# First eight projection tiles on tokens without their norm factor; smaller bias and sum matmuls, in a decoder block on one core

## The chip, the cores and the metric

One Trainium2 chip, one core. The metric is the device time of one execution of the whole program, in microseconds (us). Five engines run their own instruction lists and meet only through semaphores: PE (TensorE, matrix products), DVE (VectorE), ACT (ScalarE), POOL (GpSimd) and SP (SyncE, which here only issues DMAs).

## The reference

A decoder block on 256 tokens of width 1024, in float32:

```
xn = rmsnorm(x) * g1
proj = xn @ w_in                      # 5376 columns: GLU 1024, q, k, v 768 each, gates 2048
conv = layernorm(depthwise_conv31(a * sigmoid(gate))) -> silu -> @ w_proj
attn = dilated attention, 12 heads in 3 groups, scores + rel_bias[bucket(distance)]
h = x + (sigmoid(g_conv) * conv + sigmoid(g_attn) * attn @ w_attn) @ w_out
y = h + PEER(rmsnorm(h) * g2)         # product keys, top 16 of 128x128 experts for 8 heads
```

rmsnorm(x) is x * 1/sqrt(mean(x*x) + 1e-6), with one factor for each token.

## The kernel before

Tokens lie along the free axis: `resid` is [128, 8, 256], 8 blocks of 128 channels by 256 tokens. All weights stream through a ring of four slots of 128x1024 float32 (`raw`). Each weight tile and each right-hand side is cut into a rounded high part and a low remainder, both in the format fp32r, and a product is three matmuls: high by high, high by low, low by high. So a tile costs 24 matmuls of 128x256 (8 blocks by 3).

For a tile, SP issues its DMA when the slot is free (`load`), ACT writes the high part (`split_hi`, L312), then POOL, or DVE for every fourth tile, writes the low part (`split_lo`, L327), and PE multiplies (`product`, L1092). The order on each engine is the order of the code, and nothing overtakes. ACT splits tile n+3 in turn n of the loop over the 42 tiles of `w_in`, ahead of `evac_front(n)`, which reads result n out of PSUM. Tiles 0 to 7 give the GLU (job "glu", gate and value blocks by turns), 8 to 19 give q and k (job "qk"), then v and the gates. PSUM has eight banks; `BANK_OF` gives banks 0 to 5 to the jobs by turns, `start(job)` makes PE wait until the bank's last reader is done (`freed`), and banks 6 and 7 hold the sums of the depthwise convolution, which DVE adds tap by tap from turn 8 (`conv_tap`, L717).

The first norm stands ahead of everything: ACT squares `resid`, DVE adds pairs of blocks, PE sums over channels with a matrix of ones (job "ssq1", L1112), ACT takes the root, DVE the reciprocal. `normalise` then makes xn block by block on DVE (L671), ACT rounds it (`split_norm`, L426) and DVE takes the remainder (L666). PE starts tiles 0 and 1 side by side as the blocks come.

The bias table: 12 matmuls with 33 rows (`bias_row`, L1102) choose each head's bias row and repeat it on all 128 partitions; ACT copies each to `prob`; DMAs write it to DRAM (`toeplitz`) and read it back skewed into `bias`. The layer norm and the second RMS norm sum over channels in the same way, with 4, 4 and 8 matmuls of ones (jobs "lnsum", "lnvar", "ssq2").

After the front come 128 tiles of expert keys and 128 of expert values, with top-16 search on DVE. The change leaves their code alone.

Of the kernel before, what the change touches and what calls it, by code (L numbers as in the profile page):

```python
# [50 lines left out]
WARM_UP = 12  # L51
# [7 lines left out]
BIAS_AT = {1: (7, 8, 9), 2: (10, 11)}  # L59
# [4 lines left out]

TAPS_AT = {}
# [4 lines left out]
def jobs_in_order():  # L70

    order = [(("ssq1",), None)] + [(("bias", h), None) for h in range(7)]
    for n in range(T_CONV):
        if n < T_QK:
            order.append((("glu", n), n))
        elif n < T_V:
# [49 lines left out]
BY_DVE = ("kb", "score", "lnsum", "o", "conv", "attn", "mix")  # L126


def freed_by_dve(job):
    return job[0] in BY_DVE or (job[0] in ("glu", "pT") and job[1] % 2 == 1)  # L130

# [20 lines left out]
def hybrid_block(nc, x_t, front, cols, rel_bias, onehot, sub_keys, u_tiles, v_tiles, out):  # L152
    toeplitz = nc.dram_tensor("toeplitz", (HEADS, P * BW), F32, kind="Internal").ap()
    with ExitStack() as ctx:
# [25 lines left out]
        relb = tmp("relb", [BUCKETS + 1, HEADS, P])  # L180
# [10 lines left out]
        cu_hi = tmp("cu_hi", [P, CB, T], F32R)  # L191
        cu_lo = tmp("cu_lo", [P, CB, T], F32R)
# [6 lines left out]
        o_hi = tmp("o_hi", [P, AB, T], F32R)  # L199
        o_lo = tmp("o_lo", [P, AB, T], F32R)  # L200
# [22 lines left out]
        def part(t0, n):  # L223
# [23 lines left out]
        prm_in, rel_in, bias_out, bias_in, sk_in, y_out = [sem(s) for s in (  # L247
            "prm_in", "rel_in", "bias_out", "bias_in", "sk_in", "y_out")]
# [9 lines left out]
        relb_ready = sem("relb_ready")  # L258
# [64 lines left out]
        def split_lo(eng, base, it, j):  # L323
# [4 lines left out]
               .then_inc(lo_ready[s], 1)  # L328

# [92 lines left out]
        def _(a):  # L422
            def split_norm(k, round_):

                a.wait_ge(normed, KB * round_ + k + 1)
                a.copy(nrm_hi[:, k, :], sq[:, k, :]).then_inc(nhi, 1)  # L426

            def bias_rows(h):
                job_done(a, ("bias", h))
                a.copy(p3[:, h, :], bank[BANK_OF[("bias", h)]][:, 0:BW]).then_inc(act_evac, 1)  # L430
# [10 lines left out]
            split_hi(a, 1, 0, 0)  # L441
            for h in range(3):
                bias_rows(h)
            for k in range(KB):
                split_norm(k, 0)
                if k < 4:
                    bias_rows(3 + k)
            split_hi(a, 2, 0, 0)
# [51 lines left out]
            for n in range(T_CONV):  # L500
                split_hi(a, n + LEAD, 0, 0)
# [147 lines left out]
        def _(dve):  # L649
# [12 lines left out]
            def normalise(gain, round_):  # L662

                def lower(k):
                    dve.wait_ge(nhi, KB * round_ + k + 1)
                    dve.tensor_tensor(nrm_lo[:, k, :], sq[:, k, :], nrm_hi[:, k, :].bitcast(F32), ALU.subtract)\  # L666
                       .then_inc(nlo, 1)

                link(dve.reciprocal(rs[:, 0, 0:T], rs[:, 0, 0:T]))
                for k in range(KB):  # L670
                    dve.scalar_tensor_tensor(out=sq[:, k, :], in0=resid[:, k, :], scalar=prm[:, gain + k:gain + k + 1],  # L671
                                             in1=rs[:, 0, 0:T], op0=ALU.mult, op1=ALU.mult).then_inc(normed, 1)
                    if k:
# [4 lines left out]
            for r in range(2):
                dve.wait_ge(squared, r + 1)
                dve.tensor_tensor(sq[:, 4 * r:4 * r + 2, :], sq[:, 4 * r:4 * r + 2, :], sq[:, 4 * r + 2:4 * r + 4, :],  # L680
                                  ALU.add).then_inc(pair_sums, 1)
                if r == 0:
                    dve.wait_ge(rel_in, 32)
                    dve.wait_ge(const, 1)
                    dve.tensor_copy(relb[:, :, :], relx[:, :].unsqueeze(2).broadcast_to([BUCKETS + 1, HEADS, P]))\
                       .then_inc(relb_ready, 1)
            dve.wait_ge(prm_in, 16)
            dve.tensor_tensor(gains[:, :], prm[:, C_QG:C_QG + 1], prm[:, C_KG:C_KG + 1], ALU.mult).then_inc(gains_ready, 1)
            freed(dve, ("ssq1",))
            normalise(C_N1, 0)  # L690
            for g in range(LEAD):
                lo_of(g)

            def glu(b):

                job_done(dve, ("glu", 2 * b + 1))
                freed(dve, ("glu", 2 * b))
                dve.scalar_tensor_tensor(out=u_pad[:, b, TAPS - 1:], in0=bank[BANK_OF[("glu", 2 * b + 1)]][:, 0:T],
                                         scalar=prm[:, C_GLU + b:C_GLU + b + 1], in1=sig[:, b, :],
                                         op0=ALU.add, op1=ALU.mult).then_inc(dve_evac, 1)  # L700

            def conv_tap(w):

                for b in range(CB):
# [73 lines left out]
            for n in range(T_CONV):  # L778
                lo_of(n + LEAD)
                if n < T_QK and n % 2:  # L780
                    glu(n // 2)
# [21 lines left out]
                if n == WEIGHTS_AT + 1:  # L803
                    group_weights()
                if n == LNSUM_AT + 1:

                    job_done(dve, ("lnsum",))
                    dve.wait_ge(tap, CB * TAPS)
# [5 lines left out]
                    group_factors()  # L814
                if n > LNSUM_AT + 1:
# [45 lines left out]
            for b in range(KB):  # L861
# [3 lines left out]
                   .then_inc(dve_evac, 1)  # L865
            freed(dve, ("ssq2",))
# [611 lines left out]
```

## Time and profile before

| what | value |
|---|---|
| median of 3 runs | 1055.03 us (1053.35 to 1056.5) |
| profiled execution, its own time | 1056.55 us |
| its span (first to last instruction) | 1054.6 us |
| mean granted TensorE clock | 0.993 of 2.4 GHz |
| PE, weight load, DVE, ACT, POOL busy | 98%, 87%, 72%, 50%, 52% |

Busy shares are averages over stages with different limits. The clock of TensorE has two levels, 2.4 and 1.2 GHz, shown as 1.00 and 0.50. Matmuls are pipelined, so a PE that is busy is not always at its full rate.

### The profile page before, as it was taken

The numbers are of one execution on the slowest core, as the hardware profiler recorded it, in microseconds if no ns is written. First come the engines' busy times: TensorE is split into PE (matmuls) and PEld (weight loads), VectorE is DVE, ScalarE is ACT, GpSimd is POOL, SyncE is SP. The second block draws the span as 40 slices with busy tenths as digits, with TensorE's granted clock in tenths as the row PEclk, the third lists the DMA queues.
The fourth block names the chain that finished last, engine by engine and source line by source line (L and its number), as shares of the span: only waits on it lengthen the run. The fifth ranks groups of instructions, "written<-read, shape, count | busy, mean of one in ns | idle before, by whom it ended". The sixth has DMA issues, their size and how long they took to land.

```text
span 1054.6 us, 21139 instructions
## 1 busy us (share of the span) xinstructions
PE 1037.7 (98%) x7338; PEld 921.4 (87%) x7338; DVE 761.0 (72%) x1280; ACT 528.0 (50%) x862; POOL 551.6 (52%) x232
## 2 busy tenths in 40 slices
PE   8999998999999999999999999999999999999998
PEld 6998998999999999999888888877777778888886
DVE  5376887743299999027666666799999997777774
ACT  5454667445454444454555555544444444454453
POOL 3555562655678999984343343443443343444442
PEclk8999999999999999999999999999999999999999
DMA  5864351654545454654544554555455545556552
GB/s 192 263 224 159 108 174 62 221 179 140 180 136 179 155 188 142 216 180 160 176 164 170 173 174 161 179 178 176 162 170 174 174 161 195 188 192 199 195 188 95
DMA packets 52258, 181.91 MB, mean 172 GB/s; under 512 B 5851, under 2 KB 9051, under 8 KB 52092
## 3 DMA queue, kind: packets, MB, share of 16 engines
q1 hardware_dynamic: 52220, 181.41, 52.0%
q8 instruction: 24, 0.39, 0.2%
q14 instruction: 14, 0.11, 0.0%
HBM read 177.97 MB, written 3.41 MB: 172 GB/s over the span
## 4 chain that ended last, share of the span: by engine, by line
PE 87%; DVE 4%; issue 4%; POOL 3%; ACT 1%; DMA 1%; SPq 0%; POOLq 0%; ACTq 0%; DVEq 0%
PE bank L1385 33%; PE bank L1092 29%; PE bank L1327 11%; PE bank L1329 6%; PE bank L1341 3%; POOL lo L327 3%; PE bank L1174 2%; PE bank L1102 1%; PE bank L1303 1%; DVE nrm L1016 1%; DVE gsig L856 1%; PE bank L1251 1%; DMA relx<-rel_bias 1%; PE bank L1190 0%; PE bank L1237 0%
## 5 line engine op out<-in xcount | busy, mean ns | idle before, releaser
L327 POOL TENSOR_TENSOR lo<-raw,hi 128x1024 fp32r<-128x1024 f32 x218 | 548.7, 2527 | 488.2 <-ACT hi L312 487.8
L312 ACT CAST hi<-raw 128x1024 fp32r<-128x1024 f32 x332 | 347.8, 1048 | 203.4 <-PE bank L1385 190.9
L1092 PE MATMUL bank<-nrm,hi 128*128 128x256 f32 x1984 | 361.8, 285 | 5.6 <-POOL lo L327 3.2
L1092 PEld LDWEIGHTS bank<-nrm,hi 128*128 128x128 f32 x1984 | 310.7, 193 | 10.5 <-ACT act L577 2.9
L1385 PE MATMUL bank<-hi,nrm 128*128 128x512 f32 x1024 | 285.1, 395 | 1.4 <-DVE nrm L1016 1.4
L1092 PE MATMUL bank<-nrm,lo 128*128 128x256 f32 x992 | 281.4, 284 | 0.0
L1385 PEld LDWEIGHTS bank<-hi,nrm 128*128 128x128 f32 x1024 | 187.3, 188 | 45.5 <-DVE nrm L1016 10.1
L1016 DVE TENSOR_TENSOR nrm<-act,nrm 128x256 fp32r<-128x256 f32 x128 | 180.8, 1414 | 49.9 <-ACT nrm L609 49.9
L327 DVE TENSOR_TENSOR lo<-raw,hi 128x1024 fp32r<-128x1024 f32 x114 | 144.5, 1268 | 78.0 <-ACT hi L312 77.9
L1092 PEld LDWEIGHTS bank<-nrm,lo 128*128 128x128 f32 x992 | 191.1, 193 | 0.0
L1327 PE MATMUL bank<-nrm,hi 128*128 128x512 f32 x512 | 181.8, 399 | 0.0
L1385 PE MATMUL bank<-lo,nrm 128*128 128x512 f32 x512 | 158.2, 390 | 0.0
L1329 PE MATMUL bank<-nrm,lo 128*128 128x256 f32 x512 | 142.0, 277 | 0.0
L1327 PEld LDWEIGHTS bank<-nrm,hi 128*128 128x128 f32 x512 | 96.0, 188 | 20.8
L1385 PEld LDWEIGHTS bank<-lo,nrm 128*128 128x128 f32 x512 | 96.1, 188 | 20.5
L1329 PEld LDWEIGHTS bank<-nrm,lo 128*128 128x128 f32 x512 | 96.2, 188 | 0.0
L577 ACT ACTIVATE act<-bank 128x256 f32 x64 | 24.7, 385 | 98.0 <-PE bank L1092 97.9
L598 ACT COPY half_sum<-bank 128x256 f32<-128x256 f32 x64 | 23.9, 373 | 93.2 <-PE bank L1329 93.2
L1022 DVE TENSOR_TENSOR half_sum<-bank,half_sum 128x256 f32<-128x256 f32 x64 | 26.9, 420 | 38.2 <-ACT half_sum L598 38.2
L609 ACT CAST nrm<-act 128x256 fp32r (+1 forms) x128 | 51.2, 402 | 0.0
L997 DVE TENSOR_TENSOR ohB<-eqB,parts 128x1024 f16<-128x1024 f16 x64 | 48.0, 750 | 0.0
L717 DVE SCALAR_TENSOR_TENSOR bank<-u_pad,prm,bank 128x256 f32<-128x256 f32 x116 | 46.6, 481 | 0.0
(169 smaller groups left out, 854.8 us busy)
## 6 DMA issues: line engine op xcount, KB each, us to landing
raw<-u_tiles SPq DMA_DIRECT2D x128, 512.0 KB, 3.3
raw<-v_tiles SPq DMA_DIRECT2D x128, 512.0 KB, 3.3
raw<-front SPq DMA_DIRECT2D x76, 512.0 KB, 3.4
toeplitz<-prob SPq DMA_DIRECT2D x12, 192.0 KB, 4.3
bias<-toeplitz SPq DMA_DIRECT2D x12, 128.0 KB, 4.4
resid<-x_t SPq DMA_DIRECT2D x2, 512.0 KB, 4.7
qk<-sub_keys SPq DMA_DIRECT2D x1, 1024.0 KB, 8.2
y<-act SPq DMA_DIRECT2D x2, 512.0 KB, 2.6
```

The lines of the kernel that those rows point to most:

```text
L312: act_e.copy(hi[:, s, :], raw[:, s, :]).then_inc(hi_ready, 1)
L327: eng.tensor_tensor(lo[:, s, :], raw[:, s, :], hi[:, s, :].bitcast(F32), ALU.subtract)\
L609: a.copy(nrm_hi[:, (base_i + j) % RING, :], act[:, it * 4 + (base_i + j), :]).then_inc(a_hi, 1)
L717: dve.scalar_tensor_tensor(out=acc[:, b, :] if w == TAPS - 1 else part_sum, in0=src, scalar=wt, in1=part_sum, op0=ALU.mult, op1=ALU.add).t ...
L997: dve.tensor_tensor(ohB[:, g % 2].rearrange("p a i n b -> p (a i) n b"), eqB[:, :, :, :].unsqueeze(2).broadcast_to([P, TOK // PAIR, 2, HAL ...
L1016: dve.tensor_tensor(nrm_lo[:, s, :], act[:, it * 4 + (base_i + j), :], nrm_hi[:, s, :].bitcast(F32), ALU.subtract).then_inc(a_lo, 1)
L1022: dve.tensor_tensor(half_sum[:, j % 2, :], bank[4 + j % 2][:, 0:T], half_sum[:, j % 2, :], ALU.add)\
L1092: ins = pe.matmul(dst, w_[:, s, u * P:(u + 1) * P], x_[:, k, :], start=first and i == 0 and p_ == 0, stop=last and i == n - 1 and p_ == 2)
L1327: pe.matmul(b[:, :], hi[:, j, unit], nrm[:, k, :, :].rearrange("p a t -> p (a t)"), start=k == 0, stop=False, skip_group_check=True)
L1329: ins = pe.matmul(b[:, 0:T], lo[:, j, unit], nrm_hi[:, k, :], start=False, stop=k == KB - 1, skip_group_check=True)
L1341: ins = pe.matmul(bank[6 + g][:, q * HALF:(q + 1) * HALF], ohA[:, g, q // PAIR, :, q % PAIR], ohB[:, g, q // PAIR, i, :, q % PAIR], start= ...
L1385: ins = pe.matmul(bank[2 * c + half][:, :], a_[:, j, c * P:(c + 1) * P], v_[:, j, half * 512:(half + 1) * 512], start=False, stop=stop and ...
```

## The change

- Tiles 0 to 7 no longer wait for the norm. Their right-hand side is x times the gain g1, cut into `xg_hi` and `xg_lo` (ACT and DVE make these), and DVE multiplies each result by the token's factor when it leaves PSUM (`times_rs`). The sigmoid reads that product from SBUF.
- The sum of squares of the first norm now stands on PE behind tile 2, in 2 matmuls in place of 4. xn is made in turns 3 to 6, two blocks in each turn (`NORM_AT`), half of it by way of PSUM banks 6 and 7 (`whole`).
- DVE makes the low part of tile 1 as well (POOL did before), and reads all results of the GLU.
- The bias table takes 3 matmuls, behind tile 4, with 12 result rows each; the repetition on 128 partitions is done by three DMAs from a small DRAM table, and its DMAs come 4 or 5 tiles later in SP's list. The GLU parameters (`prm`) come by ACT's DMA queue, and the x tiles and the first weights lie first in SP's.
- DVE adds halves ahead of "lnsum" and "lnvar" (2 matmuls each), and adds up squares ahead of "ssq2" as the residual blocks come (2 matmuls in place of 8). The warm-up has 19 matmuls of ones in place of 12.

```
-WARM_UP = 12
+WARM_UP = 19
-BIAS_AT = {1: (7, 8, 9), 2: (10, 11)}
+BIAS_AT = {4: (0, 1, 2)}
+NORM_AT = {3: (0, 1), 4: (2, 3), 5: (4, 5), 6: (6, 7)}
-BY_DVE = ("kb", "score", "lnsum", "o", "conv", "attn", "mix")
+BY_DVE = ("glu", "kb", "score", "lnsum", "o", "conv", "attn", "mix")
...
 # by_dve
+            if base + j == 1:
+                return True
...
+        def whole(k, round_):
+            return sq[:, k, :] if round_ or k % 2 else bank[7][:, 0:T]
...
 # ACT, ahead of the loop
+            a.dma_start(prm[:, :], cols).then_inc(prm_in, 16)
             a.preload_act_table(ACT.Sqrt)
-            for r in range(2):
-                a.wait_ge(x_in[r], 16)
-                a.activation(sq[:, 4 * r:4 * r + 4, :], resid[:, 4 * r:4 * r + 4, :], ACT.Square)\
-                 .then_inc(squared, 1)
+            a.wait_ge(prm_in, 16)
+            a.wait_ge(x_in[0], 16)
+            for k in range(KB // 2):
+                a.activation(xg_hi[:, k, :], resid[:, k, :], ACT.Copy, scale=prm[:, C_N1 + k:C_N1 + k + 1])\
+                 .then_inc(xhi, 1)
             split_hi(a, 0, 0, 0)
+            split_hi(a, 1, 0, 0)
+            a.activation(sq[:, 0:4, :], resid[:, 0:4, :], ACT.Square).then_inc(squared, 1)
+            split_hi(a, 2, 0, 0)
...
+            split_hi(a, 3, 0, 0)
             job_done(a, ("ssq1",))
             a.activation(rs[:, 0, 0:T], bank[BANK_OF[("ssq1",)]][:, 0:T], ACT.Sqrt, bias=EPS, scale=1.0 / D)\
              .then_inc(act_evac, 1)
...
 # ACT, turn n
-                split_hi(a, n + LEAD, 0, 0)
+                if n > 0:
+                    split_hi(a, n + LEAD, 0, 0)
+                if n in NORM_AT:
+                    for k in NORM_AT[n]:
+                        split_norm(k, 0)
                 evac_front(n)
...
 # DVE
+            def x_lo(k):
+                dve.wait_ge(xhi, k + 1)
+                dve.scalar_tensor_tensor(out=xg_lo[:, k, :], in0=resid[:, k, :], scalar=prm[:, C_N1 + k:C_N1 + k + 1],
+                                         in1=xg_hi[:, k, :].bitcast(F32), op0=ALU.mult, op1=ALU.subtract)\
+                   .then_inc(xlo, 1)
...
+            def times_rs(n, to):
+                job_done(dve, ("glu", n))
+                dve.tensor_tensor(to, bank[BANK_OF[("glu", n)]][:, 0:T], rs[:, 0, 0:T], ALU.mult).then_inc(dve_evac, 1)
             def glu(b):
...
+                times_rs(2 * b + 1, u)
+                freed(dve, ("glu", 2 * b + 1))
+                dve.wait_ge(sig_ready, b + 1)
+                dve.scalar_tensor_tensor(out=u, in0=u, scalar=prm[:, C_GLU + b:C_GLU + b + 1], in1=sig[:, b, :],
+                                         op0=ALU.add, op1=ALU.mult).then_inc(glued, 1)
...
+                if b > 1:
+                    dve.wait_ge(squared, 3 + b)
+                    wait(dve, square_run, b - 2)
+                    dve.tensor_tensor(sq[:, 0, :], sq[:, 0, :], sq[:, b - 1, :], ALU.add).then_inc(square_run, 1)
...
 # PE
+            def first_tiles():
+                b0, b1, b2 = [start(("glu", n)) for n in range(3)]
+                high_products(b0, 0)
+                high_products(b1, 1)
+                low_products(b0, 0)
+                low_products(b1, 1)
+                high_products(b2, 2)
+                low_products(b2, 2)
+                b = start(("ssq1",))
+                pe.wait_ge(pair_sums, 3)
+                for k in range(2):
+                    ins = pe.matmul(b[:, 0:T], ones[:, :], sq[:, k, :], start=k == 0, stop=k == 1)
+                step(ins)
```

ACT's list around the root of the first norm, before: L439 is the root, L466 the sigmoid of tile 0, and the L312 cast that waits for pe_step and raw_in0 is the high part of tile 4.

```order
L439 ACTIVATE rs<-bank 128x256 [waits pe_step]
L312 CAST hi<-raw 128x1024 [waits raw_in1]
L430 COPY prob<-bank 128x384 [waits pe_step] x3
...
L312 CAST hi<-raw 128x1024 [waits raw_in2]
L312 CAST hi<-raw 128x1024 [waits raw_in3]
L466 ACT_TABLE_LOAD
L466 ACTIVATE sig<-bank,prm 128x256 [waits pe_step]
L312 CAST hi<-raw 128x1024 [waits pe_step,raw_in0]
```

The same place in the changed kernel, from the root (L467) on; L487 is the sigmoid, L317 the high part of a weight tile, L444 the rounding of a block of xn:

```order
L467 ACTIVATE rs<-bank 128x256 [waits pe_step]
L469 ACT_TABLE_LOAD
L487 ACTIVATE sig<-sig,prm 128x256 [waits dve_evac]
L317 CAST hi<-raw 128x1024 [waits pe_step,raw_in0]
L317 CAST hi<-raw 128x1024 [waits pe_step,raw_in1]
L487 ACTIVATE sig<-sig,prm 128x256 [waits dve_evac]
L317 CAST hi<-raw 128x1024 [waits pe_step,raw_in2]
L444 CAST nrm<-bank 128x256 [waits normed]
L444 CAST nrm<-sq 128x256 [waits normed]
```

Before, the root stood ahead of all tiles, and the first sigmoid waited only for PE. Now the first sigmoid waits for DVE's product with the factor, and the high part of tile 4 is queued behind it.

DVE's list from the low part of tile 3 to that of tile 7 in the changed kernel: L334 is a low part, L740 the product with the factor, L748 the end of a GLU block, L699 a block of xn, L691 its remainder.

```order
L334 TENSOR_TENSOR lo<-raw,hi 128x1024 [waits hi_ready]
L733 RECIPROCAL rs<-rs 128x256 [waits act_evac]
L735 COPY bank<-rs 128x256 [waits rs_ready]
L740 TENSOR_TENSOR sig<-bank,rs 128x256 [waits pe_step]
L740 TENSOR_TENSOR u_pad<-bank,rs 128x256 [waits pe_step]
L748 SCALAR_TENSOR_TENSOR u_pad<-u_pad,prm,sig 128x256 [waits sig_ready,dve_evac]
...
L691 TENSOR_TENSOR nrm<-sq,nrm 128x256 [waits nhi]
L740 TENSOR_TENSOR u_pad<-bank,rs 128x256 [waits pe_step]
L748 SCALAR_TENSOR_TENSOR u_pad<-u_pad,prm,sig 128x256 [waits sig_ready,dve_evac]
L842 COPY ksel<-ident 12x768 [waits const]
L334 TENSOR_TENSOR lo<-raw,hi 128x1024 [waits hi_ready]
```

Before, four `u_pad` instructions and three low parts were all that DVE had between xn and the taps; now the making of xn stands between them, block pair by block pair.

## Rows read from the trace of the kernel before

**Rows 1.** The page, costliest groups: line, engine, shapes, count, busy us, mean ns.

```profile
L327 DVE TENSOR_TENSOR lo<-raw,hi 128x1024 fp32r<-128x1024 f32 x114 | 144.5, 1268 | 78.0 <-ACT hi L312 77.9
```

**Rows 2.** Chain of work that ended last, first 60 us: start, length, what.

```profile
10.43 7.80 PE bank L1102 x14
18.23 7.67 PE bank L1092 x48
...
25.90 2.13 PE bank L1102 x6
...
32.58 27.43 PE bank L1092 x227
```

**Rows 3.** Timeline, first 26 us: start, length, engine, line, idle before and releaser.

```profile
1.17 4.78 PE L1107 MATMUL bank<-ones 128*128 128x128 f32 x24 [1.17 <-POOL ones L391]
...
4.86 1.06 ACT L435 ACTIVATE sq<-resid 128x1024 f32<-128x1024 f32 x1 [2.82 <-DMA resid<-x_t]
...
8.86 1.05 ACT L312 CAST hi<-raw 128x1024 fp32r<-128x1024 f32 x1 [1.31 <-DMA raw<-front]
...
9.98 4.66 POOL L327 TENSOR_TENSOR lo<-raw,hi 128x1024 fp32r<-128x1024 f32 x2 [7.58 <-ACT hi L312]
...
10.46 0.39 ACT L439 ACTIVATE rs<-bank 128x256 f32<-128x256 f32 x1 [0.56 <-PE bank L1112]
...
10.88 1.75 DVE L669 RECIPROCAL rs<-rs 128x256 f32<-128x256 f32 x1 [1.57 <-ACT rs L439]
...
12.67 2.65 DVE L671 SCALAR_TENSOR_TENSOR sq<-resid,prm,rs 128x256 f32<-128x256 f32 x2
...
15.39 0.42 DVE L666 TENSOR_TENSOR nrm<-sq,nrm 128x256 fp32r<-128x256 f32 x1
...
15.73 0.48 DVE L671 SCALAR_TENSOR_TENSOR sq<-resid,prm,rs 128x256 f32<-128x256 f32 x1
...
25.58 0.47 ACT L466 ACTIVATE sig<-bank,prm 128x256 f32<-128x256 f32 x1 [1.31 <-PE bank L1092]
```

**Rows 4.** Windows of PE: from:to, length, busy (count), granted clock, DMA.

```profile
11.00:12.00 1.00, 1.00 (x4) 0.94 0.68 270
...
21.00:22.00 1.00, 1.00 (x7) 0.50 0.00 0
22.00:23.00 1.00, 1.00 (x10) 0.94 0.00 0
...
166.00:168.00 2.00, 0.12 (x2) 1.00 0.40 100
168.00:170.00 2.00, 2.00 (x18) 0.72 0.41 162
...
172.00:174.00 2.00, 2.00 (x22) 0.93 0.00 0
```

**Rows 5.** Timeline of DVE around the layer norm.

```profile
151.13 2.06 DVE L812 TENSOR_TENSOR u_pad<-acc,rs 128x1024 f32<-128x1024 f32 x1
...
164.94 2.33 DVE L826 TENSOR_TENSOR acc<-u_pad,rs 128x1024 f32<-128x1024 f32 x1
```

**Rows 6.** Timeline of POOL around the layer norm.

```profile
149.71 5.74 POOL L327 TENSOR_TENSOR lo<-raw,hi 128x1024 fp32r<-128x1024 f32 x2 [3.13 <-ACT hi L312]
...
163.84 2.35 POOL L327 TENSOR_TENSOR lo<-raw,hi 128x1024 fp32r<-128x1024 f32 x1 [5.56 <-ACT hi L312]
```

**Rows 7.** Timeline around the second RMS norm, PE.

```profile
231.67 3.61 PE L1283 MATMUL bank<-sq,ones 128*128 128x256 f32 x16
235.12 3.73 PE L1290 MATMUL bank<-ident,resid 128*128 128x128 f32 x32
```

**Rows 8.** The same place, DVE.

```profile
231.87 0.42 DVE L864 TENSOR_TENSOR resid<-bank,resid 128x256 f32<-128x256 f32 x1 [2.45 <-PE bank L1092]
235.74 1.75 DVE L669 RECIPROCAL rs<-rs 128x256 f32<-128x256 f32 x1 [3.44 <-ACT rs L561]
```

**Rows 9.** The same place, POOL.

```profile
227.10 7.08 POOL L327 TENSOR_TENSOR lo<-raw,hi 128x1024 fp32r<-128x1024 f32 x3 [2.88 <-ACT hi L312]
```

More of the change, by code:

```diff
@@ L70, in jobs_in_order @@
 def jobs_in_order():
-    order = [(("ssq1",), None)] + [(("bias", h), None) for h in range(7)]
+    order = []
     for n in range(T_CONV):
@@ L440, in _ @@
              .then_inc(act_evac, 1)
[L441 to L448, printed above, removed]
+            a.preload_act_table(ACT.Sigmoid)
             def exp_of(s):
@@ L678, in _ @@
[L678 to L686, printed above, removed]
@@ L687, in _ @@
-            dve.wait_ge(prm_in, 16)
+                inv = rs[:, 0, 0:T] if round_ else bank[6][:, 0:T]
+                for k in ks:
+                    if round_ == 0:
+                        dve.wait_ge(rs_ready, 2)
+                        wait(dve, nlo, k - 1)
+                    dve.scalar_tensor_tensor(out=whole(k, round_), in0=resid[:, k, :],
+                                             scalar=prm[:, gain + k:gain + k + 1],
+                                             in1=inv, op0=ALU.mult, op1=ALU.mult).then_inc(normed, 1)
+                    if k > ks[0]:
+                        lower(k - 1)
@@ new lines, in _ @@
+            dve.wait_ge(x_in[1], 16)
+            for k in range(KB // 2, KB):
+                dve.tensor_scalar(xg_hi[:, k, :], resid[:, k, :], prm[:, C_N1 + k:C_N1 + k + 1], None, ALU.mult)\
+                   .then_inc(xhi, 1)
+                x_lo(k)
+            lo_of(1)
+            for i in range(2):
+                part_ = bank[6 + i][:, :].rearrange("p (k t) -> p k t", t=T)
+                dve.wait_ge(squared, 2 + i)
+                dve.tensor_tensor(part_ if i else sq[:, 0:2, :], sq[:, 2 * i:2 * i + 2, :], part_, ALU.add)\
+                   .then_inc(pair_sums, 1)
@@ L778, in _ @@
             for n in range(T_CONV):
-                lo_of(n + LEAD)
-                if n < T_QK and n % 2:
-                    glu(n // 2)
+                if n > 0:
+                    lo_of(n + LEAD)
+                if n in NORM_AT:
+                    normalise(C_N1, 0, NORM_AT[n])
+                if n < T_QK:
+                    if n % 2:
+                        glu(n // 2)
+                    else:
+                        times_rs(n, sig[:, n // 2, :])
                 for w_ in TAPS_AT.get(n, ()):
@@ L1094, in product, with full @@
                 return ins
-            def full(n, job):
+            def full(n, job, vec_hi=nrm_hi, vec_lo=nrm_lo):
                 b = start(job)
-                return product(b[:, 0:T], n % RING, [(k, k) for k in range(KB)], nrm_hi, nrm_lo, n, 0, 0)
+                return product(b[:, 0:T], n % RING, [(k, k) for k in range(KB)], vec_hi, vec_lo, n, 0, 0)
             def bias_row(h):
                 b = start(("bias", h))
-                step(pe.matmul(b[:, 0:BW], relb[:, h, :], oneh[:, h // SLOTS, :], start=True, stop=True))
+                step(pe.matmul(b[0:HEADS, 0:BW], relx[:, :], oneh[:, h, :], start=True, stop=True))
             pe.wait_ge(const, 2)
@@ L1225, in _ @@
                     b = start(("lnvar",))
[L1226 to L1228 removed]
+                    pe.wait_ge(acc_pairs, 2)
+                    for k in range(2):
+                        ins = pe.matmul(b[:, 0:T], ones[:, :], sq[:, CB + k, :], start=k == 0, stop=k == 1)
                     step(ins)
```

157 lines of the change are left out of this document (89 added, 68 removed).

## Prediction

> **What bounds the kernel now.** I read the chain of waits first, since it says which engine's work ends last in each stage. In the first 60 us it runs through PE alone from 10.43 on: seven bias matmuls, tiles 0 and 1 from 18.23, two pieces of bias work around tile 2, and from 32.58 a stretch of tiles without a gap, 24 matmuls each [rows 2]. 27.43 us for 227 gives 0.121 us a matmul and 2.9 us a tile, so tile 8, the first of q, starts at 32.58 + 5 x 2.9 = 47.0. That is the mark I measure against. From there to the layer norm PE works without a pause, so what the front gains or loses at tile 8 stands at the end. The timeline shows why tile 0 starts late: root at 10.46, reciprocal to 12.63, xn block by block after it [rows 3]. The windows show half clock from about 12 to 22 [rows 4], through the bias matmuls and half of tiles 0 and 1.
>
> Last I looked for stretched DVE instructions. L671 takes 0.48 us at 15.73, but two of them from 12.67 take 2.65 and end at 15.32, while POOL makes low parts until 14.64 [rows 3]. Both its tensors lie in SBUF, as do POOL's. The same at 164.94: 2.33 us, ending 1.08 after POOL's instruction ends at 166.19 [rows 5, 6]. So a DVE instruction with two tensors in SBUF stands still until POOL's present one ends. Reciprocal, with one, ran unstretched beside POOL at 10.88.
>
> **The first three tiles and the sum of squares.** x arrives at 4.86 as now. Weight tile 0 is ready at 8.86 now; it no longer queues behind the one-hot table, the bias table and the parameters, and 7.5 to 8.86 bounds it; I take 8.2. Its high part ends at 9.25, and PE starts there (the longer warm-up ends at about 7.5, with seven more matmuls at 0.2, or half of it at full clock, behind 5.95). DVE needs a product and a remainder for each of blocks 4 to 7, some 0.8 us a block, from about 7.0, and the last remainder meets POOL's low part of tile 0 (9.3 to 11.7) and ends at about 11.9. So PE does 14 matmuls, stands 1 us, and goes on at 11.9 with 58 more: 7.0 us to 18.9. Two sums of squares (3.61 us for eight [rows 7], 0.9 for two) end at **T = 19.7**. Low parts of tiles 1 (DVE, about 13.0) and 2 (POOL, about 15.4) and the added squares (about 15) are there in time. Were only the norm chain removed and all else hidden, this would be worth 32.58 - 19.7 = 12.9 us. Then it is given back twice.
>
> **First return: tile 4.** Its high part is queued on ACT behind the first sigmoid, and that waits for the factor. From T: root 0.39, reciprocal 1.75, copy 0.42, product 0.42, sigmoid 0.47, high part 1.05, low part 2.33, hand-overs 0.1 [rows 3]: tile 4 can start at T + 6.9. PE has tile 3 for T to T + 2.9, then stands 4.0 us.
>
> **Second return: xn.** Tile 8 wants all eight blocks. POOL works without a break on tiles 4, 5 and 6, to T + 6.9, 9.3 and 11.8. The remainder of block 1 and the GLU product of tile 3 both have two tensors in SBUF and each waits one of these out: DVE is free at T + 12.1. Then follow, each waiting for the one before: the copy to `ksel` 0.8, low part of tile 7 1.2 [rows 1], blocks 2 and 3 between DVE and ACT about 1.75 (0.48 + 0.41 + two of 0.42), product of tile 4 0.4, sigmoid 0.5, three bias copies 1.2, high part of tile 8 1.0: T + 18.8, and POOL's low part of it to T + 21.2. The remainder of block 5 waits for that end, the next GLU product waits out tile 9's (T + 23.9), and blocks 6 and 7 take 1.75: tile 8 starts at **T + 25.7 = 45.4**, 1.6 us ahead of 47.0. PE's own work is shorter: from T + 6.9 four tiles and three bias matmuls (0.7 each, from 2.13 for three [rows 2]) end at T + 20.6, so it stands some 5 us again.
>
> **The clock.** At 166 to 168 PE is nearly idle, the clock falls within the next window, and is back in 172 to 174: a grant of 0.72 over 2 us is 1.1 us at half clock, 0.93 is 0.3, and 2 us lie between, so 3.4 us at half speed or 1.7 us lost [rows 4]. I charge 1.7 once, for the stretch behind tile 8's wait; the half clock after the first stall is hidden, since PE is not the bound there. Net at tile 8: -1.6 + 1.7 = **+0.1 us**. Bounds: no fall, -1.6; and as from 12 to 22 now, where 10 us at half cost 5, if it starts among tiles 0 to 2, +5.
>
> The Trainium skill (TensorE: Matmul & The Clock Gate, Why this matters for your kernels) warns against idle gaps between bursts of matmuls, which put the clock back to 1.2 GHz. By that rule both stalls cost, not only the second. The windows at 168 agree that a gap is followed by half clock. By the rule alone the sum would rise by another 1.7 us, were PE the bound behind the first stall.
>
> **Layer norm.** DVE bounds it. Two fewer matmuls let L812 start 0.5 us sooner, but it waits for POOL's instruction that ends near 152.1, and ends at 153.2 as now. The second addition (0.7, an estimate from 1024 elements unstretched in 1.08) delays DVE, and L826 then waits for 166.19 as it does now. Sum 0; bounds -0.5 and +0.7.
>
> **Second RMS norm.** Eight matmuls in 3.61 become two in 0.9, but the addition of square 6 can start only after L864 at 232.29, has two tensors in SBUF, and POOL's three low parts run to 234.18 [rows 7 to 9]. It ends at about 234.4, and two matmuls end at 235.3, where the eight end now. Sum 0; bounds -1.5 (no wait) and +0.4. The transposes and the norm behind it last 3.7 each and move along.
>
> Later bias DMAs are hidden: they are needed by the scores near 107 us and start near 40. The experts' code follows PE and moves along, at 0.
>
> **Sum.** 1054.6 + 0.1 + 0 + 0 = 1054.7 us of span, 1056.7 of own time. The profiled execution lies 1.5 above the median of 1055.03, so the forecast for the median is **1055.2 us**.
>
> **Rivals.** *Norm pace as fast as PE.* If the two stretched instructions of DVE slip between POOL's, only tile 4's wait remains: tile 8 at T + 20.6, plus 1.7 for the clock behind the first stall, 42.0, 5 us sooner: 1050.0. For it: a shift of 0.7 us at T + 6.9 lets the remainder through. Against it: POOL has tiles 4 to 6 in a row. Chance 0.24, with all that lands between. *Half clock among the first tiles.* PE stands 1.7 us before 9.25 and 1 us at 10.9, somewhat as it stood from 5.95 to 10.43 before the fall at 12. Half clock for 3.4 to 6.8 us moves T by 1.7 to 3.4, and everything behind: 1057 to 1059; it passes the bound for slower when T is past 22.8. Chance of slower by it 0.25. *The change gains nearly all it removes*: no stall at tile 4, tile 8 near 36, 1044. The list on ACT speaks against it; 0.02. My forecast, within 0.3% (3.2 us, about what a measurement of this kernel can tell), has 0.49.
>
> Chances: faster 0.26, same 0.49, slower 0.25. Range 1049.5 to 1059.3: from just below the first rival to the end of the second.
>
> **What would show it.** Right: sums of squares on PE near 20 us; PE idle about 4 us ahead of tile 4, released by POOL's low part; stretched L691 and L748 on DVE of 1 to 2.4 us; PE idle again ahead of the first q tile near 45, released by DVE's last remainder; L1283's successor ending about 3.5 us after the last residual tile. Wrong: a first q tile at 42 or sooner, or a clock of 0.50 between 10 and 20 us.

## The result, and the profile after

| kernel | median us | range | executions |
|---|---|---|---|
| before | 1054.51 | 1053.35 to 1056.5 | 4 |
| changed | 1059.98 | 1059.34 to 1060.52 | 4 |

The ratio is 1.0050, 95% interval 1.0032 to 1.0067: slower by some 5.5 us. The changed kernel timed again in a later series gave 1059.21 against 1054.72, ratio 1.0043 (1.0030 to 1.0056). I forecast 1055.2 and "same"; the time lies outside my range.

Timeline of the changed kernel, first 26 us (columns as in rows 3):

```profile
8.96 2.63 POOL L334 TENSOR_TENSOR lo<-raw,hi 128x1024 fp32r<-128x1024 f32 x1 [6.57 <-ACT hi L317]
...
9.26 2.48 DVE L719 TENSOR_SCALAR rounded<-resid,prm 128x256 fp32r<-128x256 f32 x1
...
12.13 2.35 POOL L334 TENSOR_TENSOR lo<-raw,hi 128x1024 fp32r<-128x1024 f32 x1 [0.54 <-ACT hi L317]
12.18 2.45 DVE L719 TENSOR_SCALAR rounded<-resid,prm 128x256 fp32r<-128x256 f32 x1
...
14.67 0.48 DVE L709 SCALAR_TENSOR_TENSOR rounded<-resid,prm,rounded 128x256 fp32r<-128x256 f32 x1
...
15.21 4.21 PE L1179 MATMUL bank<-rounded,hi 128*128 128x256 f32 x18 [2.38 <-DVE rounded L709]
...
24.90 1.02 PE L1202 MATMUL bank<-sq,ones 128*128 128x256 f32 x4
```

L719 is DVE's product of x and gain for blocks 4 to 7. Two of the four take 2.48 and 2.45 us, and each ends 0.1 to 0.2 us behind a POOL instruction on weights. The last remainder (L709) ends at 15.15. I had it at 11.9. PE waits for it, and the sums of squares end at T = 25.9, where I had 19.7.

Its windows of PE (from:to, length, busy, granted clock, DMA share, GB/s):

```profile
14.00:16.00 2.00, 0.79 (x3) 0.64 0.15 61
16.00:18.00 2.00, 2.00 (x12) 0.50 0.24 68
18.00:20.00 2.00, 2.00 (x11) 0.50 1.01 337
20.00:22.00 2.00, 2.00 (x14) 0.65 0.94 332
22.00:24.00 2.00, 2.00 (x20) 1.00 0.34 135
...
52.00:54.00 2.00, 2.00 (x12) 0.53 0.96 297
54.00:56.00 2.00, 2.00 (x13) 0.62 0.97 318
```

Half clock follows the pauses from 7.2 to 15.2, and again the pause ahead of tile 8. A grant of 0.53 and 0.62 over 2 us each is 3.4 us at half clock, 1.7 us lost.

Its timeline from tile 4 to the first q tile:

```profile
30.48 7.21 POOL L334 TENSOR_TENSOR lo<-raw,hi 128x1024 fp32r<-128x1024 f32 x3 [15.99 <-ACT hi L317]
...
32.88 0.79 PE L1155 MATMUL bank<-rounded,hi 128*128 128x256 f32 x2 [4.14 <-POOL lo L334]
...
33.33 2.12 DVE L691 TENSOR_TENSOR nrm<-sq,nrm 128x256 fp32r<-128x256 f32 x1
...
35.82 2.15 DVE L748 SCALAR_TENSOR_TENSOR u_pad<-u_pad,prm,sig 128x256 f32<-128x256 f32 x1
...
44.81 2.12 DVE L691 TENSOR_TENSOR nrm<-sq,nrm 128x256 fp32r<-128x256 f32 x1
...
47.30 2.17 DVE L748 SCALAR_TENSOR_TENSOR u_pad<-u_pad,prm,sig 128x256 f32<-128x256 f32 x1
...
51.21 0.51 PE L1155 MATMUL bank<-nrm,hi 128*128 128x256 f32 x2 [2.09 <-DVE nrm L691]
```

The chain behind T is as forecast: tile 4 at T + 7.0 after a pause of 4.14 us, two stretched remainders and two stretched GLU products, and tile 8 at T + 25.3. Only PE's pause ahead of tile 8 is 2.1 us where I had some 5, since PE works at half clock behind tile 4.

The later sums, in the timeline of the changed kernel, against [rows 7 to 9]:

```profile
231.38 7.43 POOL L334 TENSOR_TENSOR lo<-raw,hi 128x1024 fp32r<-128x1024 f32 x3 [2.89 <-ACT hi L317]
...
235.77 0.42 DVE L922 TENSOR_TENSOR resid<-bank,resid 128x256 f32<-128x256 f32 x1 [1.70 <-PE bank L1155]
236.11 0.49 DVE L927 TENSOR_TENSOR sq<-sq 128x256 f32<-128x256 f32 x1
...
238.37 1.75 DVE L930 RECIPROCAL rs<-rs 128x256 f32<-128x256 f32 x1 [1.77 <-ACT rs L586]
```

From the last residual block to the reciprocal it is 2.60 us in place of 3.87 [rows 8]: 1.3 gained. For the layer norm, one row ahead of it and one behind. Before (chain of waits; timeline):

```profile
131.43 17.47 PE bank L1092 x144
```
```profile
167.88 0.88 PE L1251 MATMUL bank<-pT,v 128*64 128x128 f32 x12 [2.72 <-DVE pT L336]
```

Changed (chain; timeline):

```profile
137.21 11.73 PE bank L1155 x96
```
```profile
173.22 0.88 PE L1341 MATMUL bank<-pT,v 128*64 128x128 f32 x12 [2.60 <-DVE pT L347]
```

The lag shrinks from 5.78 to 5.34, 0.4 gained. Between the profiled spans (1057.3 and 1054.6) the account closes: tile 8 is 4.2 us later than 47.0, and the lag of 5.78 at 137.21 leaves 1.6 for the half clock behind it. Less 0.4, less 1.3, less 1.5 of the half clock at 168 to 172 [rows 4], which this execution doesn't have, is 2.6 of the 2.7 measured.

### The profile page after: what moved, and what is told of

Its sections match the earlier page's. It is cut to its first block, busy times and chain, and to the rows that moved or that the text cites. A ratio compares the mean times of both kernels' runs of the same rounds, so it can differ in the third digit from the quotient of the medians.

```text
span 1057.3 us, 21104 instructions
## 1 busy us (share of the span) xinstructions
PE 1029.0 (97%) x7310; PEld 917.1 (87%) x7310; DVE 785.3 (74%) x1310; ACT 524.6 (50%) x858; POOL 550.0 (52%) x231
## 4 chain that ended last, share of the span: by engine, by line
PE 84%; DVE 6%; issue 5%; POOL 3%; ACT 2%; DMA 0%; POOLq 0%; ACTq 0%; DVEq 0%
PE bank L1475 33%; PE bank L1155 26%; PE bank L1417 11%; PE bank L1419 6%; PE bank L1431 3%; POOL lo L334 3%; PE bank L1260 2%; PE bank L1393 1%; DVE nrm L691 1%; DVE nrm L1079 1%; DVE lo L334 1%; PE bank L1179 1%; DVE gsig L914 1%; DVE rounded L719 1%; ACT hi L317 1%
## 5 line engine op out<-in xcount | busy, mean ns | idle before, releaser
L334 POOL TENSOR_TENSOR lo<-raw,hi 128x1024 fp32r<-128x1024 f32 x217 | 547.1, 2532 | 492.6 <-ACT hi L317 492.2
L317 ACT CAST hi<-raw 128x1024 fp32r<-128x1024 f32 x332 | 347.6, 1048 | 200.1 <-PE bank L1475 190.9
L1155 PE MATMUL bank<-nrm,hi 128*128 128x256 f32 x1856 | 338.2, 285 | 7.6 <-POOL lo L334 3.2
L1155 PEld LDWEIGHTS bank<-nrm,hi 128*128 128x128 f32 x1856 | 290.5, 193 | 10.6 <-ACT act L602 2.9
L1155 PE MATMUL bank<-nrm,lo 128*128 128x256 f32 x928 | 263.2, 284 | 0.0
L334 DVE TENSOR_TENSOR lo<-raw,hi 128x1024 fp32r<-128x1024 f32 x115 | 146.8, 1276 | 73.8 <-ACT hi L317 73.7
L1155 PEld LDWEIGHTS bank<-nrm,lo 128*128 128x128 f32 x928 | 178.8, 193 | 0.0
L1419 PE MATMUL bank<-nrm,lo 128*128 128x256 f32 x512 | 142.0, 277 | 0.0
L1417 PEld LDWEIGHTS bank<-nrm,hi 128*128 128x128 f32 x512 | 96.0, 188 | 20.8
L1419 PEld LDWEIGHTS bank<-nrm,lo 128*128 128x128 f32 x512 | 96.2, 188 | 0.0
L1155 PE MATMUL bank<-rounded,hi 128*128 128x256 f32 x240 | 45.5, 292 | 4.1 <-POOL lo L334 4.1
```

Of the source, the lines that this page charges most:

```text
L317: act_e.copy(hi[:, s, :], raw[:, s, :]).then_inc(hi_ready, 1)
L334: eng.tensor_tensor(lo[:, s, :], raw[:, s, :], hi[:, s, :].bitcast(F32), ALU.subtract)\
L1155: ins = pe.matmul(dst, w_[:, s, u * P:(u + 1) * P], x_[:, k, :], start=first and i == 0 and p_ == 0, stop=last and i == n - 1 and p_ == 2)
L1417: pe.matmul(b[:, :], hi[:, j, unit], nrm[:, k, :, :].rearrange("p a t -> p (a t)"), start=k == 0, stop=False, skip_group_check=True)
L1419: ins = pe.matmul(b[:, 0:T], lo[:, j, unit], nrm_hi[:, k, :], start=False, stop=k == KB - 1, skip_group_check=True)
```

## The experiments

All on one core, each beside runs of the kernel before; ratios are to these. T is the end of the sums of squares and the first q tile is tile 8; both are read from the timeline of each profile.

| kernel | T | first q tile | median us | ratio (95%) |
|---|---|---|---|---|
| changed | 25.9 | 51.2 = T + 25.3 | 1059.98 | 1.0050 (1.0032 to 1.0067) |
| e1_pool_waits | 20.1 | 45.4 = T + 25.3 | 1053.63 | 0.9995 (0.9984 to 1.0006) |
| e2_act_all | 19.2 | 44.5 = T + 25.3 | 1054.54 | 1.0005 (0.9991 to 1.0018) |
| e3_hi4 | 26.0 | 48.8 = T + 22.9 | 1056.47 | 1.0024 (1.0015 to 1.0034) |
| e6_ssq2_old | 25.6 | 50.9 = T + 25.3 | 1060.68 | 1.0060 (1.0047 to 1.0073) |
| e7_psum_all | 24.9 | 47.0 = T + 22.1 | 1054.75 | 1.0004 (0.9995 to 1.0013) |
| e8_all | 19.7 | 39.1 = T + 19.4 | 1048.56 | 0.9949 (0.9935 to 0.9962) |
| e9_fill | 23.5 | 48.8 = T + 25.3 | 1056.55 | 1.0017 (1.0008 to 1.0027) |
| e10_sums | none | not read | 1052.38 | 0.9984 (0.9974 to 0.9994) |
| e11_early | 19.2 | 37.6 = T + 18.4 | 1048.21 | 0.9950 (0.9933 to 0.9967) |
| e12_no_hi4 | 19.5 | 41.6 = T + 22.1 | 1049.34 | 0.9949 (0.9936 to 0.9962) |
| e13_after | 25.7 | 51.0 = T + 25.3 | 1059.21 | 1.0043 (1.0030 to 1.0056) |

The theory: DVE's product of x and gain stands still behind POOL's low parts though it reads one tensor; the pauses that this makes on PE bring half clock; the list order that I had read costs the rest. The main rival is that PE was late for a reason of its own (the parameters' DMA, the clock alone).

**POOL out of the way.** POOL makes its first low part only when all remainders are there.

```
+            pool.wait_ge(xlo, KB)
             for g in range(N_FRONT + LEAD):
                 lo_of(g)
```

> The changed kernel, but POOL begins the low part of tile 0 only when the last remainder of x times gain is written, so nothing of POOL runs beside DVE's eight products and remainders. Port theory (two DVE products of 0.35 us took 2.48 and 2.45 us because POOL's low parts of tiles 0 and 2 held them up, and that made PE wait and its clock fall): last remainder at about 10.5 us instead of 15.2, PE at full clock through tiles 0 to 2, sum of squares done at 20 to 21 instead of 25.9, first q tile at 46 instead of 51.2, time 5 to 6 us below the changed kernel. Clock theory (the gap behind the warm-up alone brings the half clock, whatever DVE does): half clock again between 12 and 21, sum of squares at 23 to 24, time 2 us below.

Its timeline:

```profile
9.23 0.35 DVE L720 TENSOR_SCALAR rounded<-resid,prm 128x256 fp32r<-128x256 f32 x1
...
10.01 0.35 DVE L720 TENSOR_SCALAR rounded<-resid,prm 128x256 fp32r<-128x256 f32 x1
10.39 0.48 DVE L710 SCALAR_TENSOR_TENSOR rounded<-resid,prm,rounded 128x256 fp32r<-128x256 f32 x1
...
10.96 5.67 POOL L334 TENSOR_TENSOR lo<-raw,hi 128x1024 fp32r<-128x1024 f32 x2 [8.56 <-DVE rounded L710]
...
19.12 1.02 PE L1203 MATMUL bank<-sq,ones 128*128 128x256 f32 x4
```

All four products take 0.35 us, the last remainder ends at 10.9, the clock stays at 1.00 to 26, T is 20.1 and the time falls by 6.3 us (5.6 against the later series of the changed kernel). One added wait takes back all that the change lost. So the parameters' DMA (landed at 5.4 here too) isn't the cause.

**ACT makes all eight products**, and DVE only remainders.

```
-            for k in range(KB // 2):
+            for k in range(KB):
+                if k == KB // 2:
+                    a.wait_ge(x_in[1], 16)
                 a.activation(xg_hi[:, k, :], resid[:, k, :], ACT.Copy, scale=...)
...
-                dve.tensor_scalar(xg_hi[:, k, :], resid[:, k, :], ..., ALU.mult).then_inc(xhi, 1)
```

> The changed kernel, but ACT makes all eight rounded products of x and gain, DVE only the eight remainders; no DVE product with one source in SBUF is left beside POOL. Port theory: ACT's eight casts end at about 8.1, remainders at 9.5, before POOL's first low part has got far; first q tile near 45.5, time 5 to 6 us below the changed kernel. If instead the remainders (two sources in SBUF) are what POOL holds up and the products are not, one or two remainders still take 2.4 us, and half of the gain is missing.

T is 19.2 and tile 8 starts at 44.5, the same T + 25.3. In the trace it gains 6.7 us; its executions spread from 1052.27 to 1058.24, and the median gained 5.4. A second way around the wait gives the same answer. It doesn't tell which of DVE's instructions POOL holds up:

```profile
5.99 3.25 DVE L710 SCALAR_TENSOR_TENSOR rounded<-resid,prm,rounded 128x256 fp32r<-128x256 f32 x8 [5.99 <-ACT rounded L457]
...
9.65 2.41 POOL L334 TENSOR_TENSOR lo<-raw,hi 128x1024 fp32r<-128x1024 f32 x1 [7.26 <-ACT hi L317]
```

All eight remainders end at 9.24, before POOL's first low part starts, so neither products nor remainders meet it here.

**Only the clock.** Matmuls of ones fill PE's pauses ahead of blocks 6 and 7; DVE and POOL stay as they are.

```
-WARM_UP = 19
+WARM_UP = 27
...
                 for k in range(KB):
+                    for _ in range({6: 7, 7: 11}.get(k, 0) if n == 0 else 0):
+                        pe.matmul(bank[5][:, 0:P], ones[:, :], ones[:, :], start=True, stop=True)
                     pe.wait_ge(xlo, k + 1)
```

> The changed kernel with 8 more warm-up matmuls, and with 7 and 11 matmuls of ones ahead of the waits for the remainders of blocks 6 and 7 of tile 0, so that PE doesn't pause between 7 and 15 us. Theory (of the 6.2 us by which the sums of squares come later than forecast, 3 are half clock that follows these pauses and the rest is the late last remainder): the last remainder still ends at 15.2, the clock stays at 1.00, the sums of squares end near 23.0, everything behind moves along, median near 1057. Rival (the clock falls whether PE pauses or not, as between 12 and 22 us of the kernel before, where PE was busy): sums of squares at 25.9, median 1060.

Its timeline:

```profile
14.67 0.48 DVE L709 SCALAR_TENSOR_TENSOR rounded<-resid,prm,rounded 128x256 fp32r<-128x256 f32 x1
...
22.49 1.03 PE L1204 MATMUL bank<-sq,ones 128*128 128x256 f32 x4
```

The last remainder is as late as in the changed kernel and the clock stays at 1.00 until 30: T is 23.5 in place of 25.9. Of the 6.2 us by which T was late, 2.4 are half clock (the medians are 3.4 apart, or 2.7 against the later series). The rest is the late remainder. The profiled execution took 1060.31, the slowest of eleven, though its tile 8 starts 2.4 us sooner than in the changed kernel. Behind tile 8 it has more half clock:

```profile
50.00:52.00 2.00, 2.00 (x12) 0.50 1.02 331
52.00:54.00 2.00, 2.00 (x11) 0.50 1.03 358
```

**The high part of tile 4 ahead of the root.**

```
             split_hi(a, 3, 0, 0)
+            split_hi(a, 4, 0, 0)
             job_done(a, ("ssq1",))
...
-                if n > 0:
+                if n > 1:
                     split_hi(a, n + LEAD, 0, 0)
```

> The changed kernel, but ACT makes the high part of tile 4 ahead of the root of the norm, not behind the first sigmoid. Theory of two returns: PE no longer stands about 4 us ahead of tile 4, but the first q tile still waits for xn, whose chain on DVE and ACT behind the sum of squares shortens by only one low part on POOL: first q tile 2 to 2.5 us earlier (about 49), time 2 to 2.5 us below. Rival (the wait ahead of tile 4 is passed on whole): 4 us below. Rival (the xn chain is independent of it): no difference.

The pause ahead of tile 4 is gone, but PE then pauses 6.3 us ahead of tile 8, for DVE's last remainder, and tile 8 gains 2.4 us; the median gains 3.5. The xn chain bounds, as I had it.

**xn and the GLU products in PSUM.** The instructions that were stretched now read one tensor from PSUM. The waits that go with the shared half bank are left out here.

```
-            return sq[:, k, :] if round_ or k % 2 else bank[7][:, 0:T]
+            return sq[:, k, :] if round_ else bank[6][:, T:2 * T] if k % 2 else bank[7][:, 0:T]
...
-                times_rs(2 * b + 1, u)
+                times_rs(2 * b + 1, bank[6][:, T:2 * T])
...
-                dve.scalar_tensor_tensor(out=u, in0=u, ...
+                dve.scalar_tensor_tensor(out=u, in0=bank[6][:, T:2 * T], ...
```

> The changed kernel, with the odd blocks of xn and the first products of the GLU's value tiles in the second half of PSUM bank 6, so that the remainders of xn (L691) and the ends of the GLU blocks (L748) read one tensor from PSUM. Theory (these two-SBUF instructions stand still behind POOL's low parts): no L691 or L748 over 0.7 us, sums of squares still end at 25.9, tile 4 still waits 4.1 us, and the first q tile starts when PE is done with tile 7, near 49.2 in place of 51.2, with no half clock behind it; median near 1056.5. Rival (the making of xn is slow because ACT and DVE wait for each other block by block, and where the data lie changes nothing): first q tile at 51.2 as in the changed kernel, median 1060.

Its timeline:

```profile
31.84 0.51 PE L1159 MATMUL bank<-rounded,hi 128*128 128x256 f32 x2 [4.14 <-POOL lo L334]
31.95 0.76 DVE L691 TENSOR_TENSOR nrm<-bank,nrm 128x256 fp32r<-128x256 f32 x2 [1.82 <-ACT nrm L444]
...
33.27 0.48 DVE L752 SCALAR_TENSOR_TENSOR u_pad<-bank,prm,sig 128x256 f32<-128x256 f32 x1
...
46.98 0.40 PE L1159 MATMUL bank<-nrm,hi 128*128 128x256 f32 x2
```

No remainder takes over 0.42 and no GLU product over 0.49, while POOL works beside them; the pause ahead of tile 8 is gone. Tile 8 starts 4.2 us sooner, where I expected 2.0. Of these, 1.0 is a T of 24.9 and 1.1 is faster work from tile 4 to the end of tile 7 (15.1 us in place of 16.2), both because half clock was shorter in this execution; 2.1 is the pause itself, which is the xn chain.

**Everything at once**: the edits of e2_act_all, e3_hi4 and e7_psum_all.

> Everything at once: ACT makes all eight rounded products of x and gain, the high part of tile 4 stands ahead of the root on ACT, and xn and the GLU products lie in PSUM as in the run above. Theory (all that the front gives back is waits of DVE behind POOL, the high part of tile 4 queued behind the sigmoid, and the half clock that the pauses bring): sums of squares end at 19.2, no pause at tile 4, PE works to about 35.8, first q tile at 37 to 38, median 1045 to 1047, which is 8 to 10 us below the kernel before. Rival (the norm itself, root, reciprocal, sigmoid and eight blocks, has a pace of its own of 23 us or more behind the sums of squares): first q tile at 42 or later, median 1050 or more.

Its timeline and windows:

```profile
37.34 0.88 DVE L702 SCALAR_TENSOR_TENSOR bank<-resid,prm,bank 128x256 f32<-128x256 f32 x2
...
38.26 0.82 DVE L693 TENSOR_TENSOR nrm<-bank,nrm 128x256 fp32r<-128x256 f32 x2
...
39.13 0.51 PE L1159 MATMUL bank<-nrm,hi 128*128 128x256 f32 x2 [2.95 <-DVE nrm L693]
```
```profile
38.00:40.00 2.00, 0.87 (x7) 1.00 0.61 225
```

1048.56: 6.1 us under the kernel before and 11 under the changed one. Tile 8 starts between what the two theories had, and the time lies between them too: a pause of 2.95 us is left, since on DVE the last pair of blocks (L702 at 37.34) stands behind the end of the GLU block of tiles 4 and 5, at 37.20.

**xn a turn sooner**, on top of that, with DVE's waits moved to fit.

```
-NORM_AT = {3: (0, 1), 4: (2, 3), 5: (4, 5), 6: (6, 7)}
+NORM_AT = {3: (0, 1, 2, 3), 4: (4, 5), 5: (6, 7)}
```

> The kernel with everything at once, and xn made a turn sooner: blocks 0 to 3 in turn 3, 4 and 5 in turn 4, 6 and 7 in turn 5. Theory (what is left of the pause ahead of the first q tile, 2.95 us, is the place of the last blocks in the lists of ACT and DVE, behind the bias copies and the high part of tile 8): no pause, first q tile at 36.3, which is 16.6 us behind the sums of squares, median near 1045.7. Rival (the eight blocks have a pace of their own that the order can't change, or the earlier blocks hold up the GLU products and PE's banks): first q tile at 38.5 or later, median 1048 or more.

Its timeline and windows:

```profile
35.12 7.05 POOL L334 TENSOR_TENSOR lo<-raw,hi 128x1024 fp32r<-128x1024 f32 x3 [6.67 <-ACT hi L317]
35.33 0.76 DVE L693 TENSOR_TENSOR nrm<-bank,nrm 128x256 fp32r<-128x256 f32 x2 [2.10 <-ACT nrm L444]
...
37.62 0.67 PE L1160 MATMUL bank<-nrm,hi 128*128 128x256 f32 x2 [1.97 <-POOL lo L334]
```
```profile
38.00:40.00 2.00, 2.00 (x11) 0.50 0.76 227
40.00:42.00 2.00, 2.00 (x14) 0.71 0.54 168
```

xn is ready at 36.1, 3 us sooner, but now PE waits for POOL's low part of tile 8, whose high part stands behind the three bias copies on ACT. The pause is shorter, yet half clock follows it here, and the medians (1048.21 and 1048.56) can't be told apart. Neither theory had this wait.

**Everything at once without the early high part of tile 4.**

```
-            split_hi(a, 4, 0, 0)
             job_done(a, ("ssq1",))
...
-                if n > 1:
+                if n > 0:
                     split_hi(a, n + LEAD, 0, 0)
```

> The kernel with everything at once, but the high part of tile 4 back behind the first sigmoid. Theory (that place in ACT's list costs PE 4.1 us, and once DVE no longer waits for POOL nothing else hides it): sums of squares at 19.3, pause of 4.1 us ahead of tile 4, half clock for some 3 us behind it, first q tile near 41.5 without a pause, median near 1051, which is 2.4 above the kernel with everything at once. Rival (the pause is hidden behind the making of xn, as in the changed kernel): first q tile at 39.1, median 1048.6.

The trace bears out the theory: a pause of 4.14 us at 26.42 and tile 8 at 41.56, 2.4 us later than in e8_all. The median is 0.8 higher in place of 2.4; executions of both spread over 1.6 us and more, so the place in the list is shown by the trace and not by the time.

**The second RMS norm's sum undone**: 8 matmuls again, no additions on DVE.

> The changed kernel with the second RMS norm's sum as before: 8 matmuls, no additions on DVE. By the trace of the changed kernel (reciprocal 2.6 us behind the last residual block instead of 3.9) the additions gain 1.3 us, so this is 1.3 us above the changed kernel. By the prediction's ledger (the last addition waits for POOL's third low part) they gain nothing: no difference.

```
-            pe.wait_ge(square_run, KB - 2)
-            pe.matmul(b[:, 0:T], ones[:, :], sq[:, 0, :], start=True, stop=False)
-            pe.wait_ge(squared, 3 + KB)
-            step(pe.matmul(b[:, 0:T], ones[:, :], sq[:, KB - 1, :], start=False, stop=True))
+            for k in range(KB):
+                pe.wait_ge(squared, 3 + k + 1)
+                ins = pe.matmul(b[:, 0:T], ones[:, :], sq[:, k, :], start=k == 0, stop=k == KB - 1)
+            step(ins)
```

In the trace the reciprocal comes 3.86 us behind the last residual block (236.84 to 240.70), as before, and 1.3 later than in the changed kernel. The median is 0.7 higher than the changed kernel's 1059.98 and 1.5 higher than its later 1059.21, which brackets what the trace says.

**Only the later sums, in the kernel before**: L807, L818 and L873 on DVE are new, and three jobs have 2 matmuls each.

```
+                    dve.wait_ge(tap, CB * TAPS)
+                    dve.tensor_tensor(sq[:, CB:CB + 2, :], acc[:, 0:2, :], acc[:, 2:4, :], ALU.add)
...
+                    dve.tensor_tensor(sq[:, CB:CB + 2, :], sq[:, 0:2, :], sq[:, 2:4, :], ALU.add)
...
+                    dve.tensor_tensor(sq[:, 0, :], sq[:, 0, :], sq[:, b - 1, :], ALU.add)
```

> The kernel before with only the later sums of the change: halves added on DVE ahead of the sum and the variance of the layer norm, and squares added up on DVE ahead of the second RMS norm. Theory (the second RMS norm gains 1.3 us, and the layer norm about 0.4): reciprocal 2.6 us behind the last residual tile in place of 3.9, median 1053.0. Rival (what I forecast for it: the additions wait for POOL, both gain nothing): median 1054.7. The difference is near what five rounds can tell, so the trace decides.

The medians lie 2.2 us apart, and the ratio's interval is 0.6 to 2.7 us faster; 1.7 us was expected. In its chain of waits and its timeline the rows that answer to those around the layer norm are

```profile
128.89 11.73 PE bank L1100 x96
```
```profile
164.97 0.88 PE L1259 MATMUL bank<-pT,v 128*64 128x128 f32 x12 [3.34 <-DVE pT L337]
```

2.54 and 2.91 ahead of before: the layer norm gains 0.4, and the second RMS norm 1.3, as in the changed kernel. But 2.5 us of this trace came ahead of all that, in a front whose code is that of before. Its windows of PE:

```profile
12.00:14.00 2.00, 2.00 (x8) 1.00 0.38 113
...
16.00:18.00 2.00, 2.00 (x11) 0.56 0.91 275
18.00:20.00 2.00, 2.00 (x13) 0.58 0.32 120
```

Half clock lasts 3.4 us here where it lasted 10 in [rows 4], and the first tiles start at 15.89 in place of 18.23 [rows 2].

**The changed kernel again.**

> The changed kernel again, so that it stands beside the others of these runs with more executions. Both theories: median 1059.5 to 1060.5, sums of squares at 25.9, first q tile at 51.2.

The median is 1059.21, 0.3 us under what was expected; T is 25.7 and tile 8 starts at 51.0. In the timeline one thing differs:

```profile
12.17 2.50 POOL L334 TENSOR_TENSOR lo<-raw,hi 128x1024 fp32r<-128x1024 f32 x1 [0.64 <-ACT hi L317]
...
12.51 2.46 DVE L709 SCALAR_TENSOR_TENSOR rounded<-resid,prm,rounded 128x256 fp32r<-128x256 f32 x1
```

The last product started at 12.12, ahead of POOL's second low part, and took 0.35. The last remainder, with two tensors in SBUF, then stood behind POOL in its place and ended at 14.97, where it ended at 15.15 in the first profile. So the last block is as late whether POOL holds up its product or its remainder.

## Why the prediction was wrong

- **The step that failed is the last remainder of x times gain at 11.9, and with it T = 19.7.** I let DVE meet one low part of POOL, with the last block; it met two, with the last two blocks, and the remainder came 3.3 us later (15.15). Two things were wrong in that step. First the start times: DVE came to block 4 at 7.69 where I had 7.0, and POOL began at 8.96 where I had 9.3, so POOL's first low part already met block 6 and its second, at 12.13, met block 7. Second, the products: I took the rule from L671 and L812, with two tensors in SBUF, and costed the products, with one, as free. Two of them waited (2.48 and 2.45 us for 0.35). My ground was the reciprocal that ran unstretched beside POOL with one source; it isn't held, and the product is.
- **Which of the two errors counts.** The first is enough by itself: with free products at the measured starts, the remainder of block 6 would stand behind POOL to about 11.9 and that of block 7 to about 14.8 (an estimate from these rows and e13_after, where the second did). No run holds the remainders alone, so what the products add isn't measured apart.
- **The rule behind it.** The Trainium skill (SBUF — State Buffer, SBUF: two separate sides) says that DVE and GpSimd take one shared pair of ports as a lock, for a whole instruction, and counts among DVE's takers instructions in a two-port mode as well as those with two SBUF inputs. By that rule the trace agrees if the product ran in such a mode, which no row shows: it took 0.35 alone and 2.48 beside POOL.
- **Half clock among the first tiles** was my rival with 0.25, and it happened; a clock of 0.50 between 10 and 20 us was also one of my signs of being wrong. I had it move T by 1.7 to 3.4 us, and the kernel slower with T past 22.8; T was 25.9, of which e9_fill gives 2.4 to the clock and the rest to the remainder. The pauses that brought it were not those that I named (1.7 and 1 us) but 1.81, 1.68 and 2.38 us, the last two of them waits for DVE; e1_pool_waits, with 0.88 and 1.01, kept full clock there. And before, PE did not stand from 5.95 to 10.43, as I wrote: it made sums of squares at 6.79 and 9.30, 1.1 us each.
- **First return** (tile 4 at T + 6.9, pause 4.0): measured T + 7.0 and 4.14, and 4.1 in every kernel that keeps this place in ACT's list.
- **Second return** (tile 8 at T + 25.7): T + 25.3 in five kernels, for T from 19.2 to 25.9. e7_psum_all shows that the stretched L691 and L748 set it: with them short, PE has no pause there. My terms behind T + 12.1 add up to T + 18.95, not 18.8; nothing hangs on it.
- **Clock charge** 1.7 behind tile 8: 1.7 in the changed kernel, but none in e1_pool_waits and e2_act_all after longer pauses, and more than that in e9_fill. That it came out here is partly luck.
- **Layer norm 0**: measured -0.4, inside the bounds. The wait is as forecast: L884 ends 1.08 us behind POOL's instruction, as L826 did; but that instruction itself (169.18 in place of 163.84) came 0.4 us sooner against the chain.
- **Second RMS norm 0**: measured -1.3, near the bound -1.5. I kept POOL's three low parts where they were against the residual blocks. They began 4.77 us ahead of the last block's addition before [rows 8, 9], and 4.39 ahead in the changed kernel. With 2.5 us for each, the second then ends at 236.3, just as the addition of squares starts; it took 0.49 and not 2.1.
- **"The profiled execution lies 1.5 above the median"** was carried over to the changed kernel. But the profiled execution of before had 10 us of half clock in the front and 3.4 at 168, and a mean grant of 0.993. In the series beside e10_sums, the eight executions of before at 1056.3 to 1056.7 have 0.993 or 0.994 and the nineteen others 0.994 to 0.997, so its own 1056.55 lies with the eight. The changed kernel's profiled execution was the fastest of its four, 0.6 below their median. Of the miss of 4.8 us, 2.6 lie in the span (1057.3 against 1054.7) and 2.1 in this step.
- **Luck made the miss smaller.** At tile 8 it was 5.8 us (51.2 against 45.4). The 0.4 of the layer norm, the 1.3 of the second RMS norm and the 1.5 of half clock at 168, none of which I forecast, took it down to 2.6 in the span.

Not tried: the 3-matmul bias table alone, which is inside T and the pace behind it; and the products on ACT and the moves to PSUM in the kernel before. So how much of the 6.1 us by which e8_all is faster than before needs the rearrangement is open.

## What to carry to other kernels

Before DVE work is laid beside POOL, list for each instruction whether its sources lie in SBUF, single-source products too, and move one source to PSUM or the work to ACT; here the two, with the high part of tile 4 moved up, took 11 us off the changed kernel. Count which instructions meet the other engine's, one by one, with starts read from rows: here starts that were 0.7 and 0.3 us off would by themselves have put one more wait on DVE's list. When a chain is shortened, ask what else stands on the lists that now overlap: each wait removed here uncovered the next (product, high part of tile 4, xn, low part of tile 8). And a profiled execution has its own clock pattern: sum against several executions, or against the rows that both kernels share.

## What the runs showed of the hardware

- A DVE multiply by a per-partition scalar, 128x256 in SBUF, takes 0.35 us alone and up to 2.50 while POOL works in SBUF. With one source in PSUM, DVE's remainders and GLU products ran at 0.41 and 0.48 beside POOL (e7_psum_all).
- A pause doesn't settle the clock by its length: it stayed at 1.00 after 2.95 us (e8_all), 3.06 (e1_pool_waits) and 3.15 (e2_act_all) ahead of tile 8, and fell to 0.50 after 2.09 (changed), 1.97 (e11_early) and 3.01 (e9_fill) at the same place. What decides I can't say.
- An instruction of DVE that POOL holds up ends behind POOL's own end: a 128x256 product 0.15 us, a 128x1024 one 1.08.
- The same front code ran with 10 us of half clock in one execution and 3.4 in another, and its tiles stood 2.5 us apart. Of 27 executions of before in one series, 19 took 1053.1 to 1054.9 us and 8 took 1056.3 to 1056.7.
